# A hybrid decoder step on one core: samples' values with both groups' channels at once, and five key blocks of a prompt tile split as three and two

## The reference, cut to what matters

```python
o_c, p_c = _nsa_compressed(q, q_pos, ...)     # keys and values compressed 32 to 1
top_i, valid = _select_blocks(p_c, q_pos, ...)  # top 16 blocks of 64 keys
o_s = _sel_attend(q, ..., top_i, valid, rel_bias)
o_w = _window_banded(q, k_w, v_w, rel_bias)   # the last 512 keys
o = g[:, :, 0] * o_c + g[:, :, 1] * o_s + g[:, :, 2] * o_w
```

## Time and profile before

| | us |
|---|---|
| median of 3 runs | 914.32 (912.70 to 914.93) |
| profiled execution, device time | 913.02 |
| its span | 910.9 |
| PE busy | 863.3 (95%) |
| DVE busy | 620.5 (68%) |
| ACT busy | 368.6 (40%) |

### The profile page before, as it was taken

The page is one execution under the profiler, slowest core; times in us unless marked ns, Lnnn a source line. Parts: engine busy times, 40 slices in busy tenths (PEclk is TensorE's granted clock), DMA queues, the critical chain, the costliest instruction groups (busy, mean ns, idle before and its releaser), DMA issues.

```text
span 910.9 us, 15526 instructions
## 1 busy us (share of the span) xinstructions
PE 863.3 (95%) x5973; PEld 551.3 (61%) x5973; DVE 620.5 (68%) x1149; ACT 368.6 (40%) x878; POOL 122.6 (13%) x129
## 2 busy tenths in 40 slices
PE   6999999999999999999899998998887989999997
PEld 4666665666666666767675766765654666544442
DVE  4598788999988988998557557566775567321222
ACT  4311234311021211025777887876765656411111
POOL 0011120000001011110103131232243220000000
PEclk9999999999999999999999999999999999999999
DMA  8443651431135066540750010000029987522211
GB/s 310 173 139 119 225 197 60 54 62 55 61 121 190 27 215 219 201 138 24 273 220 1 15 79 2 2 1 1 2 93 399 359 319 292 188 103 70 81 64 41
DMA packets 32109, 118.31 MB, mean 130 GB/s; under 512 B 3433, under 2 KB 11771, under 8 KB 22971
## 3 DMA queue, kind: packets, MB, share of 16 engines
q0 software_dynamic: 9360, 68.16, 20.3%
q1 hardware_dynamic: 19053, 43.39, 13.8%
q10 hardware_dynamic: 3623, 5.76, 3.0%
HBM read 108.33 MB, written 13.29 MB: 134 GB/s over the span
## 4 chain that ended last, share of the span: by engine, by line
PE 78%; DVE 11%; DVEq 3%; ACT 3%; issue 2%; DMA 1%; another core or an unknown queue 0%; ACTq 0%; POOL 0%; POOLq 0%
PE PS L836 28%; PE PS L2181 12%; PE PS L1616 6%; PE PS L1626 6%; PE PS L1644 5%; PE PS L812 3%; PE PS L2000 3%; DVE main L609 3%; PE PS L2061 2%; ACT main L1417 2%; PE PS L2025 2%; PE PS L2038 2%; DVE main L606 2%; PE PS L1599 1%; PE PS L801 1%
## 5 line engine op out<-in xcount | busy, mean ns | idle before, releaser
L836 PE MATMUL PS<-main 128*128 128x352 f32 (+1 forms) x1056 | 328.0, 469 | 0.0
L836 PEld LDWEIGHTS PS<-main 128*128 128x128 f32 x1056 | 200.4, 191 | 119.6 <-issue 1.5
L1417 ACT ACTIVATE main<-PS,main 128x512 f32<-128x512 f32 (+3 forms) x192 | 104.0, 562 | 48.7 <-DVE main L1457 24.5
L2181 PE MATMUL PS<-main 128*128 128x512 f32 x256 | 111.6, 593 | 0.0
L437 ACT ACTIVATE main<-PS 128x384 f32<-128x384 f32 x24 | 11.8, 490 | 201.7 <-PE PS L836 195.5
L1626 PE MATMUL PS<-cst,main 128*128 128x128 f32 x528 | 73.7, 282 | 15.0 <-ACT main L1417 12.5
L647 DVE SCALAR_TENSOR_TENSOR main<-main,par 128x1022 f32<-128x1022 f32 (+16 forms) x66 | 83.8, 1270 | 5.3 <-issue 0.4
L606 DVE TENSOR_TENSOR main<-main 128x1024 f32<-128x1024 f32 x64 | 75.4, 1220 | 11.6 <-DMA main<-in_cmp_k_dram,row 7.9
L2181 PEld LDWEIGHTS PS<-main 128*128 128x128 f32 x256 | 47.9, 190 | 58.1 <-issue 58.0
L609 DVE TENSOR_TENSOR main<-main 128x1024 f32<-128x1024 f32 (+2 forms) x96 | 75.0, 781 | 7.2
L1626 PEld LDWEIGHTS PS<-cst,main 128*128 128x128 f32 x528 | 57.7, 142 | 30.2 <-ACT main L1417 22.8
(11 more groups left out here) (320 smaller groups left out, 1032.1 us busy)
## 6 DMA issues: line engine op xcount, KB each, us to landing
main<-in_w_tiles_dram SPq DMA_DIRECT2D x24, 512.0 KB, 3.6
out_dram<-main SPq DMA_DIRECT2D x18, 256.0 KB, 2.1
main<-in_x_prompt_dram SPq DMA_DIRECT2D x8, 512.0 KB, 8.4
main<-in_w_out_dram SPq DMA_DIRECT2D x4, 1024.0 KB, 7.8
main<-in_x_prompt_dram SPq DMA_DIRECT2D x16, 256.0 KB, 3.0
out_dram<-main SPq DMA_DIRECT2D x4, 512.0 KB
diag<-in_win_k_dram SPq DMA_DIRECT2D x8, 256.0 KB
diag<-in_win_v_dram SPq DMA_DIRECT2D x8, 256.0 KB
```

The source lines that it names most:

```text
L836: last = pe.matmul(bank(3 * s + j)[:, 0:w], ring[:, s, k * P:(k + 1) * P], xT[:, k, t0:t0 + w], start=(k == 0), stop=(k == KD - 1))
L1417: last = act.activation(prob[:, k % 2, g, h * nk_ * P:(h + 1) * nk_ * P], score_set(k, g)[:, h * nk_ * P:(h + 1) * nk_ * P], ACT.Exp, scal ...
L2181: last = pe.matmul(out_bank(m, h), proj[:, MIX[k], n * P:(n + 1) * P], wo[:, k, h * 512:(h + 1) * 512], start=(x == 0), stop=(x == KD - 1))
```

## The change

For tiles 4 to 7 the five blocks of the window are split as three (with the edge mask on the first of them) and two, instead of one and four. Tile 4's selected branch, which also has five blocks, is split as three far and two near, instead of one and four. The list that brought edge parts of neighbouring tiles together is gone: parts follow in their order. There are 74 steps instead of 69 and 37 batches instead of 35. The fused minimum is now also used where a group holds two heads of two blocks (256 columns each, one instruction a head), which includes tile 1; where bias is added apart, it is added to the last two blocks only.

In the samples' part the values, compressed blocks and new tokens are multiplied once per sample with the channels of both groups: 64 stationary columns (both groups' rows) and 128 moving ones. A row then holds its own group's result and one of the other group, which nothing reads: `gate` takes each group's rows from its own channels. The accumulators in the PSUM bank are 128 columns wide instead of 64, and `finish` works on 128 columns. The new tokens' matmuls (L2070, not shown in the diff) change as those of the compressed blocks do. In the first round the key copy of odd chunks is divided: ACT does sample 0 in an extra instruction, DVE sample 1.

```diff
...
@@ -1316,8 +1316,10 @@
             else:
-                parts = [(0, 0, i - 3, "far"), (0, i - 3, 4, "near"), (1, i - 4, 1, "edge"), (1, i - 3, 4, "near")]
-            order = [0, 1, 3, 2] if i in (5, 7) else [2, 0, 1, 3] if i == 6 else [2, 1, 3, 0] if i == 4 else [0, 1]
+                split = i - 3 if i > 4 else 3
+                parts = [(0, 0, split, "far"), (0, split, i + 1 - split, "near"), (1, i - 4, 3, "edge"), (1, i - 1, 2, "near")]
+            order = range(len(parts))
             for c in order:
@@ -1451,21 +1453,22 @@
                     h = 1 + g * R + r0
-                    if heads == 1 and kind == "near":
-                        if n == 512:
-                            v = s.rearrange("p (a n) -> p a n", a=2)
-                            dve.tensor_tensor_reduce(v, v, diag[:, 0:h + 1:h, :], 1.0, BIG, ALU.add, ALU.min, m).then_inc(SEM["s_max"], 1)
-                        else:
-                            dve.tensor_tensor(s[:, n - 2 * P:], s[:, n - 2 * P:], diag[:, h, :], ALU.add)
-                            dve.drain()
-                            dve.tensor_reduce(m, s, X, ALU.min).then_inc(SEM["s_max"], 1)
+                    v = s.rearrange("p (h n) -> p h n", h=heads)
+                    if kind == "near" and n == 512 and heads <= 2:
+                        for j in range(heads):
+                            one = v[:, j, :].rearrange("p (a n) -> p a n", n=2 * P)
+                            add = diag[:, 0:h + 1:h, :] if heads == 1 else diag[:, h + j:h + j + 1, :]
+                            last = dve.tensor_tensor_reduce(one, one, add, 1.0, BIG, ALU.add, ALU.min, m[:, j:j + 1])
+                        last.then_inc(SEM["s_max"], 1)
                     else:
-                        v = s.rearrange("p (h n) -> p h n", h=heads)
                         if kind == "near":
-                            dve.tensor_tensor(v, v, diag[:, h:h + heads, 2 * P - nk_ * P:], ALU.add)
+                            w = min(nk_, 2) * P
+                            e = v[:, :, nk_ * P - w:]
+                            dve.tensor_tensor(e, e, diag[:, h:h + heads, 2 * P - w:], ALU.add)
                             dve.drain()
                         if kind == "edge":
-                            dve.tensor_tensor(v, v, c_("winmask").rearrange("p (o n) -> p o n", o=1).to_broadcast([P, heads, P]), ALU.add)
+                            dve.tensor_tensor(v[:, :, 0:P], v[:, :, 0:P], c_("winmask").rearrange("p (o n) -> p o n", o=1).to_broadcast([P, heads, P]), ALU.add)
                             dve.drain()
@@ -1742,8 +1745,12 @@
             o = bank(6 + p % 2)
-            return o[:, 0:HD], o[:, HD:2 * HD], o[:, 2 * HD:3 * HD], o[:, 3 * HD:3 * HD + P], o[:, 3 * HD + P:3 * HD + P + 2 * DS]
+            return o[:, 0:P], o[:, P:2 * P], o[:, 2 * P:3 * P], o[:, 3 * P:4 * P], o[:, 2 * P:2 * P + 2 * DS]
+        def sample_rows(b2):
+            return slice(b2 * Q, (b2 + 1) * Q)
@@ -1847,6 +1854,9 @@
                     if swapped(c):
+                        if r == 0 and b2 == 0:
+                            act.activation(o[HD:2 * HD], i[0:HD], ACT.Copy)
@@ -1933,13 +1943,11 @@
                 values_used(dve, p, NC + 1)
-                dve.tensor_scalar(osb1, window, sm[:, 45:46], None, ALU.mult)
+                dve.tensor_scalar(osb, window, sm[:, 45:46], None, ALU.mult)
                 dve.drain()
-                dve.scalar_tensor_tensor(osb1, pages, sm[:, 44:45], osb1, ALU.mult, ALU.add)
+                dve.scalar_tensor_tensor(osb, pages, sm[:, 44:45], osb, ALU.mult, ALU.add)
                 dve.drain()
-
-                dve.tensor_tensor(osb.rearrange("p (k d) -> p k d", k=2), osb1.rearrange("p (o d) -> p o d", o=1).to_broadcast([P, 2, HD]),
-                                  blocks.rearrange("p (o d) -> p o d", o=1).to_broadcast([P, 2, HD]), ALU.add).then_inc(SEM["o_sb"], 1)
+                dve.tensor_tensor(osb, osb, blocks, ALU.add).then_inc(SEM["o_sb"], 1)
@@ -1954,7 +1962,9 @@
                     dve.wait_ge(SEM["sd_ps"], k - 3)
-                dve.tensor_copy(ktc[HD:2 * HD, k % 4].rearrange("p b n -> p (b n)"), keys_bank(r, c, 0, 2)[0:HD]).then_inc(SEM["kt_dve"], 1)
+                first = 1 if r == 0 else 0
+                dve.tensor_copy(ktc[HD:2 * HD, k % 4, first:].rearrange("p b n -> p (b n)"),
+                                keys_bank(r, c, first, 2 - first)[0:HD]).then_inc(SEM["kt_dve"], 1)
@@ -2046,8 +2056,8 @@
                     pe.wait_ge(SEM["dpair"], p - 1)
-                for b2, g, q in QUARTERS:
-                    pe.matmul(gather(p)[2][q:q + 32, :], ptd[:, p * P + q:p * P + q + 32], vcn[:, 2 * p + b2, g * HD:(g + 1) * HD], start=True, stop=True)
+                for b2 in range(2):
+                    pe.matmul(gather(p)[2][sample_rows(b2), :], ptd[:, p * P + b2 * Q:p * P + (b2 + 1) * Q], vcn[:, 2 * p + b2, :], start=True, stop=True)
@@ -2055,10 +2065,10 @@
                     for j in range(4):
-                        for b2, g, q in QUARTERS:
+                        for b2 in range(2):
                             at_ = (4 * c + j) * P % 2048
                             v = values_half(p, c // (NC // 2))[:, b2, at_:at_ + P] if c < NC else vw_d[:, b2, j * P:(j + 1) * P]
-                            last = pe.matmul(gather(p)[0 if c < NC else 1][q:q + 32, :], ptd2[:, c % 2, j * P + q:j * P + q + 32], v[:, g * HD:(g + 1) * HD],
+                            last = pe.matmul(gather(p)[0 if c < NC else 1][sample_rows(b2), :], ptd2[:, c % 2, j * P + b2 * Q:j * P + (b2 + 1) * Q], v,
                                              start=(c in (0, NC) and j == 0), stop=False)
...
```

More of the change, by code:

```diff
@@ L976, in program @@
         mask2 = kcn_flat[:, 640:768]
-        osb, osb1 = kcn_flat[:, 768:896], kcn_flat[:, 896:960]
+        osb = kcn_flat[:, 768:896]
         gd = sb("gd", [P, 4, 3])
@@ L2068, in new_values @@
                 pe.wait_ge(dp_sb[c % 2], p_par(p, c) + 1)
-                for b2, g, q in QUARTERS:
-                    last = pe.matmul(gather(p)[k][q:q + 32, :], ptd2[0:2 * DS, c % 2, k * P + q:k * P + q + 32],
-                                     vn[0:2 * DS, (2 * p + b2) * P + g * HD:(2 * p + b2) * P + (g + 1) * HD], start=False, stop=True)
+                for b2 in range(2):
+                    last = pe.matmul(gather(p)[k][sample_rows(b2), :], ptd2[0:2 * DS, c % 2, k * P + b2 * Q:k * P + (b2 + 1) * Q],
+                                     vn[0:2 * DS, (2 * p + b2) * P:(2 * p + b2 + 1) * P], start=False, stop=True)
                 if k == 1:
```

## The result

The changed kernel takes 918.55 us (median of 20 executions, 916.47 to 920.51), the kernel before 914.45 us beside it (20 executions). The ratio is 1.0047, 95% interval 1.0037 to 1.0056: some 4 us slower, where 6.3 were forecast.

The account below looks back on a forecast made before the run. TensorE, busy 95% of the span, was taken as the bound. Terms of +6.5, -0.8 and +0.6 us gave +6.3: 919.3 us from the profiled 913.0, an expected median of 920.5, range 909 to 931.

Parts of the forecast that it names:

- Part A: Samples' values: two matmuls of 64 stationary and 128 moving columns instead of four of 32 and 64; +6.5 us.
- the key copy: First sample round: VectorE's key copy halved, one more ScalarE copy for four chunks; -0.8 us, bounds +2.4 and -2.4.
- two terms: Samples' values on TensorE: added work of +16.0 us, against it instruction gaps of which 9.5 of 10.7 us return.
- Rival 1: Samples' value runs: gaps follow loaded DMA engines, not demand, and stay, saving about 1 us; 929 us, chance 0.15.
- Overhead per matmul: Samples' value runs: the skill's 60 cycles would make the work an estimated +5 us; rejected for the trace's 16 ns a record.
- Part B: Prompt's attention: five blocks split as three and two, gains and losses by stretch nearly cancelling; +0.6 us.
- The half clock at 483 to 487 us: Prompt, after the first edge batch: clock fall following an idle stretch, about 2 us, expected gone.
- Rival 2: Prompt's three-block masks keep up; rounds fall to TensorE's own 4.6 and 5.25 us, 17 us less; 904 us, chance 0.12.
- the three terms: Whole kernel: samples' values +6.5, divided key copy -0.8, five blocks as three and two +0.6; sum +6.3 us.

Follow-up runs that it names:

- a_light: `a_values` with the page loads of sample pairs 3 and 4 cut to 256 of 2048 columns, only time read; 919.68 us, 1.0065 of the kernel before.
- light: Kernel before, page loads of sample pairs 3 and 4 cut to 256 of 2048 columns, only time read; 903.71 us, ratio 0.9922.
- wide_quarters: Changed kernel with four value matmuls of 32 stationary columns, each with all 128 moving columns, in place of two; 916.25 us, 1.0049 of the kernel before.
- k_copy: Kernel before with only the key copy of odd chunks in the first sample round divided between ScalarE and VectorE; 910.66 us, ratio 0.9996.
- a_values: Kernel before with the samples' values, compressed blocks and new tokens in the new shape, key copy undivided; 916.8 us, ratio 1.006.
- tile1_fused: Kernel before with the new code of the minima but the old split, so only tile 1 changes; 907.91 us, ratio 0.9968.
- b_fused: Kernel before with the three-and-two split and the edge step's mask addition and minimum in one instruction; 906.84 us, 0.9957; again 905.42 us, 0.9934.

## Why the prediction was right

- **Part A** was forecast at +6.5 us before the key copy and measured at +5.6 in traces and 1.006 in time. Its two terms hold. The work was +16.0, of which 32 records in 1.90 us is exact; behind the first run the terms make 15.1, and `a_light` less `light` gives 16.1 without the excess, 1.0 more than I worked out. Of the gaps I expected 9.5 of 10.7 us back: behind the first run 9.0 us of excess became 1.0. What I gave as the reason for the second, demand rather than packets, is what `wide_quarters` shows. There was luck in this size: I counted gaps inside value runs only, and the profile that I read has nearly all of them there, 9.0 us behind the first run, where `k_copy` has 4.2 of a stretch that is as long. The Trainium skill (Runtime: NRT & Kernel Launch, Instruction fetch mechanics) holds the crossing of a block "mostly hidden". If the gaps are such crossings, which is inferred, they are hidden in `a_values` (0.1 us of excess), and in the earlier trace rows (10.7 us) they are not.
- **Rival 1** (gaps stay, 929) named the right condition, loaded DMA engines, and drew the wrong end from it: at 34 instructions per microsecond under full load there is 0.1 us of excess in `a_values` and 1.0 in after.
- **Overhead per matmul.** The Trainium skill (TensorEngine Tiling (Array Packing), Instruction Overhead) gives each matmul some 60 cycles of overhead, an estimated 25 ns at 2.4 GHz. The runs have 16 ns a record for quarters at 64 columns, below it, and 29.5 at 128 (1.89 us for 64). So going by the row was right: the rule's +5 us for the work of part A would have been wrong by 11.
- **The key copy**, forecast at -0.8: 0.6 us less in its round in `k_copy` and `wide_quarters`, 0.1 in after, and nothing in the time (0.9996). This term failed: VectorE's copy sets less of that round than I took, and I did not name the wait behind it, the key pages' DMA.
- **Part B**, forecast at +0.6: -0.1 in the region and 1.0022 in time, whose interval holds both 0 and +0.6 us. By stretch: 23.92 (24.06 forecast), 17.78 (17.86), 60.66 (60.95), 13.50 (13.65); edge rounds 5.65 (5.68), two-block rounds 6.48 (6.5). The half clock at 483 to 487 us is gone, as said. The four experiments with the old split and the old minima have it, as before had; none of the seven profiles with the new split has such a fall in the region of part B. `tile1_fused`, with the old split, has it behind the other edge batch (0.79 over 555 to 563 us), so all six profiles with the old split have one. At the first one the starts of TensorE's groups from 474 to 483 us are as in before to 0.01 us, shifted by 0.17, and yet the clock falls in before only (timeline of PE, before and then `tile1_fused`):

```profile
483.02 2.55 PE L1616 MATMUL PS<-main 64*128 64x384 f32 x8
482.85 1.56 PE L1617 MATMUL PS<-main 64*128 64x384 f32 x8
```

That round takes 6.47 us in `tile1_fused` instead of 7.99, so the fall cost 1.5 us, where I had put about 2. What decides between the two places is open, so a cause of the fall, the idle stretch before it or another, is not shown.

- **Rival 2** (masks keep up) put the gain where it is, in VectorE's 0.84 us a step; the fused edge is the case in which they do, and its edge rounds of 4.84 and 4.51 us stand beside the 4.6 that it named for them. The other half of the rival, two-block rounds at 5.25, did not come: they stay at 6.49 in `b_fused`, so it gains 7.8 us and not 17.
- **What is not accounted for.** The two profiled spans differ by 7.4 us: 5.5 in the samples' rounds, -0.1 in part B's region, and 2.1 that after loses ahead of its fifth batch (462.54 against 464.62), in code that the change does not touch. Over all thirteen profiles that batch starts between 462.24 and 464.62 us, in two of one and the same kernel (`b_fused`) at 464.29 and 462.39, so this part is a difference between executions. The medians differ by 4.1. By the windows of before and after the three terms come to 5.5 - 0.1 - 0.1 = 5.3 us in place of 6.3; the medians' interval, 3.4 to 5.1, ends a little lower, and why is open. The parts measured alone, +5.5, +2.0 and -0.4 us, add up to more than the whole, within their intervals.

## What to carry to other kernels

When a busy engine has gaps inside a run of tiny instructions, price the wider shape by its bare work first: here fewer, wider matmuls got some 10 us of gaps back (10.7 became 1.0) and paid 16 for them. Gaps that a profile ends with "issue" can stand before other instructions in the next profile, so compare the whole stretch and not one group. Before splitting work evenly for balance, look at the latency chain of the smaller batch (minimum, exponential, turn): it was the pitch of the slowest step on that chain, 0.84 us, that set the round, and fusing two instructions was worth more than the balance. And take a bundle apart: one term of it (the fused minimum in tile 1) was a gain of 3.8 us that the others hid.

## What the runs showed of the hardware

- Four matmul streams of 32 stationary columns each beside one another take 16 ns a record at 64 moving columns and 29.5 ns at 128; two of 64 stationary columns take 59 ns at 128 (1.90 us for 32). At 128 columns both forms produce results at the same rate.
- TensorE's gaps in such streams depended on both the rate (under full load, 124 instructions per microsecond: 9.0 us of excess in before, 4.2 in `k_copy`; 68: 1.4; 34: 0.1 to 1.0) and, at the highest rate, on the DMA share (0.76: 9.0; 0.43: 2.8). At 34 a lower share did not lower them (0.38: 1.9).
- VectorE's fused addition and minimum repeats every 0.52 us over 384 columns and, in `b_fused`, one is 461 ns long over 256 columns, 589 over 384 and 727 over 512: its length falls with its columns, and the short form was worth using (3.8 us in tile 1). The row of the 256-column form, over 440 to 640 us:

```profile
L1463 DVE CUSTOM_DVE_ANT_0 PS<-PS,cst 128x256 f32<-128x256 f32 x40 | 15.5, 461 | 10.6 <-PE PS L1624 10.6
```
